# Narrow projections of a hybrid decoder layer as a stage of their own, ahead of the recurrent steps

## What is computed

```python
    q_g, k_g, v_g, r_g, lr_g, q_a, k_a, v_a, gate_a, gate_b = jnp.split(h @ w_in, idx, axis=-1)
    q_g = q_g.reshape(n, t, GLA_HEADS, GLA_DK) * (GLA_DK ** -0.5)
...
    log_a = (jax.nn.log_sigmoid((lr_g @ gk_up + gk_bias).astype(jnp.float32)) / GLA_TAU)
...
    o_g, s_new = gla_run(q_g, k_g, v_g, log_a, s0, GLA_CHUNK, (-N_META) % GLA_CHUNK)
    o_a = swa_prompt(q_a, k_a, v_a, rel_bias, sinks)
...
    y_g = gla_output(o_g, r_g, gla_norm_g)
    merged = jax.nn.sigmoid(gate_a) * y_g + jax.nn.sigmoid(gate_b) * o_a.astype(h.dtype)
    h1 = layer_norm(ALPHA * h + merged @ w_out, ln1_g, ln1_b)
    f = hier_moe(h1.reshape(n * t, d), w_rg, b_rg, w_re, b_re, w_gate, w_up, w_down).reshape(n, t, d)
```

## Time and profile before

| | |
|---|---|
| median of 3 runs | 2064.47 us (2063.5 to 2065.47) |
| profiled execution | 2060.25 us, its span 2058.3 us |
| mean granted TensorE clock | 0.946 |
| TensorE busy | 1861.7 us (90%) |
| VectorE, ScalarE, GpSimd busy | 58%, 40%, 15% |
| recurrent stage | 93.4 to 1075.3 us, 36 steps |

### The profile page before, as it was taken

How to read it: one execution, slowest core, us unless ns; L and a number is a source line. 1 busy time by engine, 2 the same in 40 slices (tenths; PEclk the granted TensorE clock), 3 DMA queues, 4 the chain that set the end, 5 groups by cost and what they waited for, 6 DMA issues and landing times.

```text
span 2058.3 us, 29998 instructions
## 1 busy us (share of the span) xinstructions
PE 1861.7 (90%) x10358; PEld 1533.3 (74%) x10358; DVE 1195.3 (58%) x1710; ACT 829.7 (40%) x1501; POOL 303.0 (15%) x320
## 2 busy tenths in 40 slices
PE   4599999999999999999998799429999999999965
PEld 3488888888888888888874688427777777777742
DVE  4365556555565555655555233566777877777716
ACT  2343334333343333433321122306666666666623
POOL 2211112111111111211110011230000000000025
PEclk9899999999999999999997699659999999999988
DMA  5810006000060002400027822647999999999954
GB/s 211 274 58 27 27 17 184 27 27 17 14 183 27 27 27 59 142 27 19 22 87 252 273 92 92 235 148 276 399 398 397 399 399 399 398 397 399 372 189 179
DMA packets 177466, 370.20 MB, mean 180 GB/s; under 512 B 22080, under 2 KB 67856, under 8 KB 177208
## 3 DMA queue, kind: packets, MB, share of 16 engines
q1 hardware_dynamic: 162864, 320.75, 43.4%
q0 software_dynamic: 9968, 32.35, 4.1%
q10 hardware_dynamic: 4608, 16.78, 2.0%
HBM read 320.49 MB, written 59.67 MB: 185 GB/s over the span
## 4 chain that ended last, share of the span: by engine, by line
PE 80%; issue 9%; DVE 6%; DMA 2%; POOL 2%; ACT 2%; POOLq 0%; SPq 0%; ACTq 0%; DVEq 0%
PE PS L1750 15%; PE PS L1701 14%; PE PS L1702 14%; PE PS L1703 14%; PE PS L1995 5%; PE PS L1708 2%; PE PS L1826 2%; PE PS L1788 2%; PE PS L1825 1%; PE PS L1789 1%; PE PS L1851 1%; PE PS L1858 1%; PE PS L1808 1%; PE PS L1815 1%; PE PS L1817 1%
## 5 line engine op out<-in xcount | busy, mean ns | idle before, releaser
L1568 DVE TENSOR_TENSOR wm_lo<-raw,wm_hi 128x2048 fp32r<-128x2048 f32 x156 | 352.1, 2290 | 146.3 <-ACT wm_hi L1132 146.3
L1750 PE MATMUL PS<-hT,wn 128*128 128x128 f32 x2880 | 334.1, 278 | 0.0
L1132 ACT CAST wm_hi<-raw 128x2048 fp32r<-128x2048 f32 x160 | 301.8, 1907 | 74.3 <-PE PS L1703 74.2
L1750 PEld LDWEIGHTS PS<-hT,wn 128*128 128x128 f32 x2880 | 327.2, 193 | 4.4 <-issue 0.2
L1701 PE MATMUL PS<-w_hi,hT_hl 128*128 128x512 f32 x576 | 234.8, 408 | 6.8 <-DVE hT_hl L1270 4.7
L1702 PE MATMUL PS<-w_lo,hT_hl 128*128 128x512 f32 x576 | 227.8, 396 | 0.0
L1703 PE MATMUL PS<-w_hi,hT_hl 128*128 128x512 f32 x576 | 227.8, 396 | 0.0
L1701 PE MATMUL PS<-wm_hi,xT_hi 128*128 128x512 f32 x512 | 203.9, 398 | 3.1 <-DVE xT_lo L1633 3.1
L1703 PE MATMUL PS<-wm_hi,xT_lo 128*128 128x512 f32 x512 | 201.0, 393 | 0.0
L1702 PE MATMUL PS<-wm_lo,xT_hi 128*128 128x512 f32 x512 | 200.6, 392 | 0.0
L1324 DVE SCALAR_TENSOR_TENSOR Sc<-PS,bias 128x512 f32<-128x512 f32 (+1 forms) x72 | 44.2, 655 | 198.7 <-PE PS L1789 198.7
(11 more groups left out here) (331 smaller groups left out, 3108.3 us busy)
## 6 DMA issues: line engine op xcount, KB each, us to landing
raw<-in_w_gate SPq DMA_DIRECT2D x64, 1024.0 KB, 9.5
raw<-in_w_up SPq DMA_DIRECT2D x64, 1024.0 KB, 10.3
raw<-in_w_down SPq DMA_DIRECT2D x64, 1024.0 KB, 10.5
hT<-hT_dram SPq DMA_DIRECT2D x36, 512.0 KB, 3.3
braw<-in_w_in SPq DMA_DIRECT2D x16, 1024.0 KB, 11.1
obuf_dram<-yb ACTq DMA_DIRECT2D x32, 512.0 KB, 6.9
obuf_dram<-h_dram SPq DMA_DIRECT2D x2, 4608.0 KB, 24.6
h_dram<-hn SPq DMA_DIRECT2D x9, 512.0 KB, 6.0
```

Source lines behind the costliest of these rows:

```text
L1132: act.copy(wm_hi[:, j], raw[:, j]).then_inc(m_hi[j // 4], 1)
L1568: dve.tensor_tensor(wm_lo[:, j], raw[:, j], BF(wm_hi[:, j]), ALU.subtract).then_inc(m_lo[j // 4], 1)
L1750: last = pe.matmul(out, wn[:, k, c:c + P], hT(k), start=(k == 0), stop=(k == KC - 1))
```

## The change

The narrow projections leave the steps. They become 75 units of TensorE work, begun during the embedding (`project`): 15 for each group (five products by three thirds of 384 tokens, `T3`), three for the low rank, and 12 for the gate. The activations are split in the embedding, straight from PSUM (`xa_hi`, `xa_lo`), and stay in SBUF for all units; the narrow weights are split too. A unit is 8 slices by three matmuls with a weight tile stationary and 384 tokens moving. ScalarE copies each result to `ev` and stores it to `nd_dram`. The split activations are stored to `hl_dram`.

A step loads its narrow results from `nd_dram` (SP's queue, `nd` and `ka`) and its split activations from `hl_dram` (GpSimd's queue, `hT_hl`, one step ahead). The split of `hT`, the copies of `xg`, `ka`, `vT` and `qa` disappear. The wide weights get three half slots: two pieces of the next group are split inside step 7, one in step 8, the fourth in the first step. Groups are unrolled; the inner loop covers steps 1 to 6. Nearly all waits of a step become `wait_apart`.

```diff
+    def half_slot(g, j):
+
+        return (2 * g + j // 2) % 3
...
+        def hT_load(b, s, n):
+            if not (isinstance(n, int) and n < 2):
+                wait_apart(pool, b_gg, upto(n - 2))
+            for i in range(2):
+                pool.dma_start(hT_hl[s][:, i], hl_dram[ds(b, 1), i].rearrange("o p n -> p (o n)")).then_inc(b_hp[s], 16)
...
+            def step(n, b, s, uses, first):
+                if not (isinstance(n, int) and n == G * NB - 1):
+                    hT_load((b + 1) % NB if isinstance(b, int) else b + 1, 1 - s, n + 1)
...
+                for j in pieces:
+                    wide(g + 1, j)
...
+        def project(*unit):
+
+            kind, g, c, tc = unit
+            m = number[unit]
+            if m >= 3:
+                pe.wait_ge(n_ev, m - 2)
+            out = PS[:, 3 + m % 3, 0:T3]
+            if kind == "gk":
+                pe.wait_ge(b_gk, 32)
+                pe.wait_ge(n_ev, number[("lr", 0, 0, tc)] + 1)
+                last = pe.matmul(out, gkup[:, g * DK:(g + 1) * DK], lrT[:, tc * T3:(tc + 1) * T3], start=True, stop=True)
+            else:
+                r = 0 if kind == "lr" else 1 + 5 * g + c
+                pe.wait_ge(n_wlo, r + 1)
+                pe.wait_ge(e_lo, upto(3 * tc + 2))
+                hi, lo = chunk(r)
+                for k in range(KC):
+                    pe.matmul(out, hi[:, k], xa_hi[:, tc, k], start=(k == 0), stop=False)
+                    pe.matmul(out, hi[:, k], xa_lo[:, tc, k], start=False, stop=False)
+                    last = pe.matmul(out, lo[:, k], xa_hi[:, tc, k], start=False, stop=(k == KC - 1))
+            last.then_inc(n_acc, 1)
+
+        for b in range(3):
+            e_transposes(b)
+        for tc in range(3):
+            project("lr", 0, 0, tc)
+            for c in range(5):
+                project("nd", 0, c, tc)
+                if c < 3 and tc < 2:
+                    e_transposes(3 * tc + 3 + c)
+            for g in range(G):
+                project("gk", g, 5, tc)
+        for g in range(1, G):
+            for c in range(5):
+                for tc in range(3):
+                    project("nd", g, c, tc)
...
-                pe.wait_ge(b_hT[s], 16 * (uses + 1))
-                pe.wait_ge(b_va, upto(n - 1))
-                pe.matmul(PS[:, 5, P:2 * P], gkup[:], lrT[:, ds(b * P, P)], start=True, stop=True)
-                feature_major(PS[:, 5, 0:P], W_KV).then_inc(b_p5, 1)
-                pe.wait_ge(b_qq, upto(n - 1))
-                feature_major(PS[:, 4, 0:P], W_Q)
-                feature_major(PS[:, 4, P:2 * P], W_K)
-                feature_major(PS[:, 4, 2 * P:3 * P], W_QA)
-                feature_major(PS[:, 4, 3 * P:4 * P], W_QA + P).then_inc(b_p4, 1)
-                wait_apart(pe, b_ka, upto(n))
-                pe.transpose(PS[:, 5, 2 * P:2 * P + HD], vT[HD:P, :], ident[HD:P, HD:P]).then_inc(b_vt, 1)
-                pe.wait_ge(b_hl, upto(n))
+                if not (isinstance(n, int) and n == 0):
+                    wait_apart(pe, b_hp[s], 32 * loads)
                 if first:
...
+                    pe.wait_ge(n_ev, len(units))
+                wide(PS[:, 2], 0).then_inc(b_vr, 1)
+
+                wait_apart(pe, b_nd[s], 16 * (uses + 1))
+                wait_apart(pe, b_kd, 32 * (n + 1))
+                wait_apart(pe, b_pc, upto(n - 1))
+                wait_apart(pe, b_pd, upto(n - 1))
+                for c in range(2):
+                    for keys in ((1 - s, s) if not first else (s,)):
+                        for half in range(2):
+                            r = slice(half * HD, (half + 1) * HD)
+                            k0 = c * 2 * P + (P if keys == s else 0)
+                            last = pe.matmul(PS[:, half, k0:k0 + P], nd[s][r, 2 + c, :], ka[keys][r, :], start=True, stop=True)
                 last.then_inc(b_sc, 1)
...
+                for j in pieces:
+                    wide(g + 1, j)
+
+                wait_apart(dve, b_pt, upto(n))
                 dve.tensor_copy(Pt[:, 1].rearrange("p h q -> p (h q)"), PS[:, 1]).then_inc(b_pd, 1)
```

More of the change, by code:

```diff
@@ new lines, in build @@
+    padW2 = sb(sW, "padW2", [P, 184])
+    braw = sb(sW, "braw", [P, 2, KC, 256])
+    hT_hl = [sb(sW, f"hT_hl{s}", [P, 2, D], F32R) for s in range(2)]
+    sink = sb(sW, "sink", [P, HEADS])
+    ax = sb(sW, "ax", [P, P])
+    mn = sb(sW, "mn", [P, P])
+    g16 = sb(sW, "g16", [P, P])
+    b16 = sb(sW, "b16", [P, P])
+    bm = sb(sW, "bm", [P, 2])
+    eq = sb(sW, "eq", [P, P])
+    ek = sb(sW, "ek", [P, P])
+    ebm = sb(sW, "ebm", [P, 1])
+    e2 = sb(sW, "e2", [P, 1])
+    At = sb(sW, "At", [P, P])
@@ L552, in bias_loads @@
+        wide_load(0, 1)
+        for r in range(11, 15):
+            raw_load(r)
+        wide_load(0, 2)
+        wide_load(0, 3)
+        for r in range(15, 21):
+            raw_load(r)
         def bias_loads(g):
@@ L968, in _ @@
[L968 to L980 removed]
+        e_hT(1)
+        high(3)
+        first(3, 1)
+        e_hT(2)
+        high(4)
+        first(4, 0)
+        high(5)
+        act.wait_ge(b_gk, 32)
+        evacuate("lr", 0, 0, 0)
+        evacuate("nd", 0, 0, 0)
@@ new lines, in _ @@
+        e_hT(3)
+        first(5, 1)
+        evacuate("nd", 0, 1, 0)
+        e_hT(4)
+        first(6, 0)
+        evacuate("nd", 0, 2, 0)
+        e_hT(5)
+        evacuate("nd", 0, 3, 0)
+        first(7, 1)
+        evacuate("nd", 0, 4, 0)
+        for g in range(G):
+            evacuate("gk", g, 5, 0)
+        evacuate("lr", 0, 0, 1)
+        evacuate("nd", 0, 0, 1)
+        e_hT(6)
+        first(8, 0)
+        evacuate("nd", 0, 1, 1)
+        e_hT(7)
+        evacuate("nd", 0, 2, 1)
+        e_hT(8)
@@ new lines, in step @@
+            def step(n, s, uses, first, pieces=()):
+                if first and g:
+                    wide(g, 3)
+                wait_apart(act, b_nd[s], 16 * (uses + 1))
+                wait_apart(act, b_g16, upto(n - 1))
+                act.activation(ax[:], nd[s][:, 5], ACT.Abs).then_inc(b_ax, 1)
+                wait_apart(act, b_ax, upto(n))
+                act.activation(ax[:], ax[:], ACT.Exp, scale=-1.0).then_inc(b_ex, 1)
+                wait_apart(act, b_ex, upto(n))
+                act.activation(ax[:], ax[:], ACT.Ln, bias=1.0).then_inc(b_lx, 1)
+                wait_apart(act, b_bmn, upto(n))
+                wait_apart(act, b_qq, upto(n - 1))
+                wait_apart(act, b_Sm, upto(n - 1))
+                wait_apart(act, b_e2, upto(n - 1))
+                if first:
+                    act.activation(gse[:, g], g16[:, 0:NS], ACT.Exp, scale=1.0 / TAU)
@@ L1251, in _ @@
+        low(0)
+        low(1)
+        e_next(1)
+        low(2)
+        e_next(2)
+        e_low(0)
+        low(3)
+        e_next(3)
+        e_low(1)
+        low(4)
+        e_low(2)
+        e_next(4)
+        low(5)
+        e_next(5)
+        e_low(3)
+        e_next(6)
+        e_low(4)
+        e_low(5)
+        e_next(7)
+        e_next(8)
+        e_low(6)
         e_scale(8, 0)
+        e_low(7)
+        e_low(8)
+        for r in (6, 7, 8):
+            low(r)
         stage0_done(dve)
+        for u in range(5, 20):
+            if u + 4 < 21:
+                low(u + 4)
+            if u in (7, 9, 11, 13):
+                wide(0, (u - 7) // 2)
@@ new lines, in _, with step, wide @@
+        for g in range(G):
+            n0 = g * NB
+            def step(n, s, uses, loads, first):
+                if isinstance(n, int) and n == 0:
+                    x_hi = lambda k: xa_hi[:, 0, k, 0:P]
+                    x_lo = lambda k: xa_lo[:, 0, k, 0:P]
+                else:
+                    x_hi = lambda k: hT_hl[s][:, 0, k * P:(k + 1) * P]
+                    x_lo = lambda k: hT_hl[s][:, 1, k * P:(k + 1) * P]
+                def wide(out, j):
+                    t = half_slot(g, j)
```

802 lines of the change are left out of this document (411 added, 391 removed).

## The result

The changed kernel takes **2070.71 us** (median of 13 runs, 2066.53 to 2076.94) against 2064.47 (median of 13 runs beside it): a ratio of 1.0035, 95% interval 1.0027 to 1.0043. The forecast was 2045; the change is a small loss.

A forecast was written before the change was run, and what follows sets the result against it. TensorE, busy 99% of the stage of steps, was taken to bound the kernel. Narrow stage 347, first step 23.8, 35 steps of 18.4 (644) and boundaries 41 made 1056 against 1075.3, hence 2045 us against 2064.47; range 2008 to 2092.

The forecast's parts named there:

- Each wait an instruction more: In the step's loop, about ten separate waits at 0.03 us each, between 0 and 0.06, lengthen a step from 18.1 to 18.4.
- the boundaries: At group boundaries, steps 7 and 8, the first step and the next add 13.6 us together, three times: 41.
- the narrow stage: Narrow products ahead of the steps: 63 units of 4.3 us, passes of 0.18 us, ending at 347 us.
- the gate chain: VectorE's mn, g and scan in each step: 1.94 us, bounding the step at 18.1 us, by 0.45.
- the chain is longer than I count: Rival: steps above 18.95 us make a loss; at 19.2 to 19.5 the kernel takes 2073 to 2084; chance 0.17.
- TensorE's own step: TensorE's work in a step without the narrow products: 17.65 us.
- steps at TensorE's bound: Rival: steps of 17.65 us without contention on mn and scan, narrow pass 0.175: 2011, or 2019 with steps alone; chance 0.14.
- First steps: Each group's first step: Sc waits for GpSimd's bias copy until about T + 16, making 23.3 us, +5.
- The last step: The last of the 36 steps, counted like an ordinary one at 18.4 us.
- late-loads rival: Rival: hT halves land more than 4 us later and stop TensorE every step; 3 us past that gives 2150; chance 0.05.
- The granted clock: TensorE's clock: full in the steps; about 3 us allowed for half-clock stretches before the narrow stage's first group ends.
- the long step 7: Step 7 of a group: two weight splits ahead of the Pt copy on VectorE delay Pt to 21.3, +5.0 us.

The follow-up runs named there:

- e10: Changed kernel with only VectorE's waits of the steps made plain again, as in the kernel before: 2040.0 us, ratio 0.9872 to the kernel before.
- e11: Changed kernel with only TensorE's and ScalarE's waits of the steps made plain again: 2068.35 us, ratio 1.002 to the kernel before.
- e1: Changed kernel with the next step's gate chain made one step early: 2024.71 us, ratio 0.9816 to the kernel before.
- e5: Changed kernel with GpSimd's hT loads and bias copy put ahead of the output stores at a group's end: 2063.96 us, ratio 0.9999 to the kernel before.
- e9: Changed kernel with the sample-cache copies issued behind the last step's gate product: 2071.6 us, ratio 1.0042 to the kernel before.
- e2: Changed kernel with six idle TensorE products ahead of kk.qq in each step: 2080.98 us, ratio 1.0082 to the kernel before.
- e8: Changed kernel with early gate chain, bias copy first, weight pieces spread, sample copies last and the steps' waits plain: 1961.29 us, ratio 0.9504 to the kernel before.

## Why the prediction was wrong

**The step that failed: "Each wait an instruction more".** The prediction took 0.03 us for each of ten hops, 0.3 a step, and 0.06 as the bound, which it had from TensorE's weight queue, another engine's. The runs show 0.89 a step for VectorE's waits alone (e10), 30.7 us for the kernel; on TensorE and ScalarE the same edit is worth 2.4 at most (e11). The bound was near what a hop shows (0.06), the 0.03 was not, and there were more than ten: the kernel has twenty such waits on VectorE from the first `Et` operation to `kk`, and more in the softmax. The 0.59 a step that the sum lacked is 20.6 us over 35 steps, more than the 19 that it forecast to gain. Without VectorE's separate waits the changed kernel takes 2040, 24 us below the kernel before: the forecast's side. That it is within 5 us of the forecast's number is in part luck, as other terms cancel there: the boundaries were dearer, the narrow stage and the gate chain cheaper (below).

**The rival that happened** is "the chain is longer than I count": steps above 18.95 make a loss, and ordinary steps came to 19.05. Its price, 2073 to 2084, begins 2 us above what was measured; its second part, more contention on `mn`, did not come (below).

**Terms of the sum that were mis-sized**, the largest first:
- *TensorE's own step* is 16.8 (e1), not 17.65, so that TensorE is at kk.qq earlier and waits 1.4 to 2.0, not 0.5. Most of the difference (0.64) is the score products: 16 passes from 390.80 to 391.80 above, where the kernel before, by the lines below, takes from 519.75 to 521.39. The prediction took their time over from before, but the diff also changes their order (the two halves of 64 rows now alternate from pass to pass); that the order does it was not tried by itself. A shorter TensorE step alone doesn't change a step that the chain bounds, but with the gate chain out of the way such steps reached 16.8, below the 17.65 of the rival "steps at TensorE's bound".

```profile
519.75 0.49 PE L1788 MATMUL PS<-ka,qa 64*128 64x128 f32 x2
...
521.39 0.49 PE L1796 MATMUL PS<-qq,kk 128*128 128x128 f32 x2
```

- *The gate chain* was taken at 1.94 from `mn` to scan's end; it is 1.63 in the step shown (390.07 to 391.70) and 1.66 in the mean of the inner steps: `mn` now takes the short time of the earlier trace rows in all of them, the scan in most (0.76 to 0.89 in seven of twenty), and `g` is the long one instead (0.80 here). This pays back 0.3 of the waits' 0.89.
- *The narrow stage* was 10 us too dear. Passes of 384 columns start 0.173 apart (TensorE's timeline below), below the 0.18 taken and nearly three quarters of a 512-column pass. The Trainium skill, "TensorE: Matmul & The Clock Gate", section "Back-to-back issue gap", would make it 162.5 ns, an estimate from that page; the trace stays above that, as the prediction weighed it.

```profile
199.98 0.34 PE L1923 MATMUL PS<-xa_hi,wn 128*128 128x384 f32 x1
200.15 0.34 PE L1924 MATMUL PS<-xa_lo,wn 128*128 128x384 f32 x1
```

- *First steps* had the right wait, and at one of three boundaries the wrong landing. The bias was taken to be there at T + 16 (T is PV's end) with a store landing of 1.96; at the boundary shown it came at T + 19.8, by a landing of 5.57, and that step (28.65) has 5.35 of the 7.0 by which the three missed. e5 takes the stores and their landing off the path and wins 6.8.
- *The last step* waits 5.0 us for its halves. The copies of the sample caches, issued ahead of them, are what held them up (e9). The loads landed in 5.5 us in the median, 2.2 more than the 3.3 taken, and the spare of 4 us held in every other step: no other step waited for its halves, so the price of the late-loads rival did not come. What makes up the 2.2 was not tried.
- *The granted clock* was taken as 1.00 throughout the steps. It is 0.93, some 104 us at the 1.2 GHz level (0.07 x 2 x 746.6). In the inner steps it costs little (e2: 3.5 us in 20 steps). Most of it lies around the boundaries, and what it costs there was not measured apart.

**What held:** TensorE at the narrow products for good at 57; evacuations and splits hidden there; the loop that bounds a step, and TensorE waiting for `qq` (with a small wait for the softmax beside it, one of the prediction's signs of being wrong); the long step 7 (`Pt` behind two splits: 18.7 us of waits, six times) and step 8; no late halves but one.

**Still open:** the first step of the stage, 27.0 instead of 23.8, was not tried by itself, and of the first steps' remaining length over 16.8 only the wait behind `qq` in e8 is known (11.9 in four).

## What to carry to other kernels

Work taken off the busiest engine is worth only what it exceeds the chain that it covered: time that chain first, hop by hop, on each engine's own timeline, idle time between short operations included. A wait of its own is cheap on an engine that waits anyway and dear in a chain of short operations. When the cover goes, start the dependent chain a step early and spread queued work over the steps: these two, with the bias copy put first and the sample copies last, turned a loss of 0.35% into a gain of 4.5%, and plain waits made it 5.0%.
